# A hybrid decoder step on one core: expert weights in 2 MiB transfers of 16 KB per partition, a ring of 8 places, and a gather of full height

## The reference

```python
def expert_block(args):
    xb, e = args
    g = jnp.minimum(xb @ lp['w_gate'][e] + lp['b_gate'][e], SWIGLU_LIMIT)
    u = jnp.clip(xb @ lp['w_up'][e] + lp['b_up'][e], -SWIGLU_LIMIT, SWIGLU_LIMIT)
    act = g * jax.nn.sigmoid(SWIGLU_ALPHA * g) * (u + 1.0)
    return act @ lp['w_down'][e] + lp['b_down'][e]
```

## Time and profile before

| what | us |
|---|---|
| median of 3 runs (1362.7 to 1371.55) | 1368.54 |
| the profiled execution | 1360.56 |
| its span, first to last instruction | 1358.5 |

### The profile page before, as it was taken

The page is one execution under the profiler, slowest core; times in us unless marked ns, Lnnn a source line. Parts: engine busy times, 40 slices in busy tenths (PEclk is TensorE's granted clock), DMA queues, the critical chain, the costliest instruction groups (busy, mean ns, idle before and its releaser), DMA issues.

```text
span 1358.5 us, 15076 instructions
## 1 busy us (share of the span) xinstructions
PE 1278.8 (94%) x5901; PEld 588.4 (43%) x5902; DVE 316.2 (23%) x674; ACT 154.6 (11%) x253; POOL 35.2 (3%) x43
## 2 busy tenths in 40 slices
PE   5999979789999999999999999999999999999895
PEld 2653646454343534434353444434343434434332
DVE  2232462422021202112120211212120211112114
ACT  1331231210110001001000101000000101000001
POOL 0010232000000000000000000000000000000000
PEclk8899987868999999999999999999999999999988
DMA  9354767509899999999999999999999999999971
GB/s 375 155 195 135 279 240 292 228 12 407 352 410 408 409 409 409 409 410 410 409 409 410 410 409 409 410 410 409 410 410 410 409 410 409 409 409 409 410 295 40
DMA packets 125029, 477.53 MB, mean 352 GB/s; under 512 B 7360, under 2 KB 9536, under 8 KB 124736
## 3 DMA queue, kind: packets, MB, share of 16 engines
q1 hardware_dynamic: 124672, 474.41, 88.2%
q0 software_dynamic: 320, 2.60, 0.5%
HBM read 473.07 MB, written 3.91 MB: 351 GB/s over the span
## 4 chain that ended last, share of the span: by engine, by line
PE 81%; DMA 13%; DVE 3%; ACT 2%; issue 1%; DVEq 0%; ACTq 0%
PE ps L508 80%; DMA arena<-in_w_up 11%; ACT arena L1081 2%; DVE arena L1137 1%; DMA arena<-in_w_in 1%; DMA arena<-in_w_ada 1%; PE ps L856 0%; DMA arena<-in_xT 0%; PE ps L746 0%; DVE arena L1566 0%; DVE arena L1344 0%; DVE arena L1143 0%; DVE arena L1341 0%; DVE arena L1564 0%; PE ps L790 0%
## 5 line engine op out<-in xcount | busy, mean ns | idle before, releaser
L508 PE MATMUL ps<-arena 128*64 128x512 f32 (+7 forms) x5648 | 1244.3, 527 | 64.2 <-DVE arena L1137 24.3
L508 PEld LDWEIGHTS ps<-arena 128*64 128x64 f32 (+2 forms) x5648 | 557.0, 159 | 741.7 <-issue 625.1
L1081 ACT ACTIVATE arena<-ps 128x1024 f32<-128x1024 f32 x51 | 52.3, 1025 | 635.1 <-PE ps L508 618.1
L1137 DVE TENSOR_TENSOR arena<-arena,ps 128x320 f32<-128x320 f32 (+2 forms) x140 | 69.1, 494 | 162.6 <-PE ps L508 156.6
L1447 DVE TENSOR_SCALAR arena<-ps 128x1024 f32<-128x1024 f32 x17 | 20.8, 1224 | 348.3 <-PE ps L508 348.3
L1137 DVE TENSOR_TENSOR arena<-arena 128x1024 f32<-128x1024 f32 (+12 forms) x90 | 75.0, 858 | 79.0 <-ACT arena L1009 32.5
L1451 DVE TENSOR_SCALAR arena<-ps 128x1024 f32<-128x1024 f32 x17 | 20.8, 1225 | 207.7 <-PE ps L508 207.7
L1089 ACT ACTIVATE arena<-arena 128x1024 f32<-128x1024 f32 x17 | 18.0, 1060 | 281.9 <-DVE arena L1447 281.9
L1432 DVE TENSOR_SCALAR arena<-arena 128x64 f32<-128x64 f32 (+1 forms) x102 | 24.4, 305 | 1.8 <-issue 1.8
L1439 DVE COPY arena<-arena 128x64 f32 (+1 forms) x34 | 5.4, 193 | 78.1 <-PE ps L508 78.1
L821 PE MATMUL ps<-arena 128*128 128x128 f32 x136 | 19.2, 286 | 2.7 <-DVE arena L1452 2.7
(11 more groups left out here) (119 smaller groups left out, 155.0 us busy)
## 6 DMA issues: line engine op xcount, KB each, us to landing
arena<-in_w_gate SPq DMA_DIRECT2D x136, 1024.0 KB, 18.3
arena<-in_w_up SPq DMA_DIRECT2D x136, 1024.0 KB, 18.3
arena<-in_w_down SPq DMA_DIRECT2D x136, 1024.0 KB, 18.4
arena<-in_w_ada SPq DMA_DIRECT2D x24, 1024.0 KB, 7.6
arena<-in_w_in SPq DMA_DIRECT2D x10, 1024.0 KB, 11.7
arena<-in_w_out SPq DMA_DIRECT2D x4, 1024.0 KB, 8.0
arena<-in_s0T SPq DMA_DIRECT2D x1, 2048.0 KB, 9.6
out_ssmsT<-arena POOLq DMA_DIRECT2D x1, 2048.0 KB, 6.5
```

Of the source, the lines that this page charges most:

```text
L508: return pe.matmul(o, l, r, start=start, stop=stop, skip_group_check=True)
L1081: A(moe[name].rearrange("p (a b) -> p a b", a=2), ps[:, bank:bank + 2, :], ACT.Copy).then_inc(done, 1)
L1137: return V.tensor_tensor(o, a, b, op)
```

## The change

Three things change. The weights are laid out on the host so that each load is one contiguous piece per partition: 8 KB for a front unit (`w_front`), 16 KB for an expert load (`w_exp`). An expert load is now 2 MiB, half of a matrix, four chunks of 128 rows (CHUNKS); the ring has 8 places instead of 16, of the same 16 MiB, PER is 12, and a product waits for its loads, and frees them, in two halves instead of four quarters. And the gather's third tile is 128 rows high: the rows above 64 of `htok` and `sel` are set to zero once, by GpSimd at its start and by DVE before the router's result.

```diff
 UNIT = 2048
-RING = 16
 FS = 6
-PER = 24
+CHUNKS = 4
+LOAD = CHUNKS * D
+RING = 8
+HELD = FS * UNIT // LOAD
+PER = 3 * 2 * KC // CHUNKS
...
-        ring, ring_at = sb([RING, UNIT])
+        ring, ring_at = sb([RING, LOAD])
+        front = view(ring_at, [FS, UNIT])
...
         def exp_slot(j, k):
-            return (FS + PER * j + k) % RING
+            return (HELD + PER * j + k) % RING

         def exp_source(k, e):

-            m, p = k // 8, k // 2 % 4
-            return w_exp[m][bass.ds(e(k % 2), 1), :, 2 * p:2 * p + 2, :].rearrange("e p c n -> p (e c) n")
+            return w_exp[bass.ds(e(k % 2), 1), k // 2].rearrange("e p n -> p (e n)")
...
-                slot = ring[:, u % FS, :]
-                src = front_source(m, j)
-                sp.dma_start(slot.rearrange("p (c n) -> p c n", c=src.shape[1]), src).then_inc(front_landed[u % FS], 16)
+                sp.dma_start(front[:, u % FS, :], w_front[u]).then_inc(front_landed[u % FS], 16)

             def load_unit(k, e, slot):
-                sp.dma_start(ring[:, slot, :].rearrange("p (c n) -> p c n", c=2), exp_source(k, e)).then_inc(exp_landed[slot], 16)
+                sp.dma_start(ring[:, slot, :], exp_source(k, e)).then_inc(exp_landed[slot], 16)
...
                 for k in range(KC):
-                    for t, (t0, n) in enumerate(TILES):
-                        last = mm(ps[:, 6 + k // 4, (k % 4) * P:(k % 4 + 1) * P], htok[0:n, t, k * P:(k + 1) * P],
-                                  moe["sel"][0:n, t, :], t == 0, t == NT - 1)
+                    for t in range(NT):
+                        last = mm(ps[:, 6 + k // 4, (k % 4) * P:(k % 4 + 1) * P], htok[:, t, k * P:(k + 1) * P],
+                                  moe["sel"][:, t, :], t == 0, t == NT - 1)
                 last.then_inc(x_mm, 1)
...
-                for p in range(4):
+                for p in range(KC // CHUNKS):
                     for s in range(2):
                         pe.wait_ge(exp_landed[slots[2 * p + s]], loads[2 * p + s])
-                    w = [ring[:, slots[2 * p + s], :].rearrange("p (c n) -> p c n", c=2) for s in range(2)]
-                    for kk in range(2):
+                    w = [ring[:, slots[2 * p + s], :].rearrange("p (c n) -> p c n", c=CHUNKS) for s in range(2)]
+                    for kk in range(CHUNKS):
...
-                                if kk == 1 and half == 1:
+                                if kk == CHUNKS - 1 and half == 1:
                                     last.then_inc(exp_used, 1)
...
             pe.wait_ge(htok_ready, NT)
+            pe.wait_ge(pad_zero, 1)
             gather(0)
...
+            step(V.memset(moe["sel"][TS:P, 2, :], 0.0))
             step(V.memset(logit, 0.0))
...
                     if not last:
-                        dve.wait_ge(exp_used, q * PER + 17)
+                        dve.wait_ge(exp_used, q * PER + 2 * PER // 3 + 1)
                         pick_bias(lambda s: (q + 1) * 2 + s)
...
             step(Q.memset(line[:, :, 0:PAD], 0.0))
+            Q.memset(htok[TS:P, 2, :], 0.0).then_inc(pad_zero, 1)
+            pool.wait_ge(pad_zero, 1)
...
+    w_exp = np.stack([a[n][0] for n in ("w_gate", "w_up", "w_down")], axis=1)
+    w_exp = w_exp.reshape(NE, PER // 2, CHUNKS, P, D).transpose(0, 1, 3, 2, 4).reshape(NE, PER // 2, P, LOAD)
```

More of the change, by code:

```diff
@@ L282, in scratch @@
             up[0] += n
-            assert up[0] <= ring_at + RING * UNIT
+            assert up[0] <= ring_at + RING * LOAD
             return view(at, shape)
@@ L385, in build @@
         moe_zero = sem("moe_zero")
+        pad_zero = sem("pad_zero")
         sel_ready, selw_ready, pick_ready, x_mm, x_ready = (
@@ L393, in build @@
         dve_steps, act_steps, pool_steps = sem("dve_steps"), sem("act_steps"), sem("pool_steps")
[L395 to L410, removed]
+        w_front = d["w_front"]
+        w_exp = d["w_exp"]
         def exp_slot(j, k):
-            return (FS + PER * j + k) % RING
+            return (HELD + PER * j + k) % RING
         def exp_source(k, e):
-            m, p = k // 8, k // 2 % 4
-            return w_exp[m][bass.ds(e(k % 2), 1), :, 2 * p:2 * p + 2, :].rearrange("e p c n -> p (e c) n")
+            return w_exp[bass.ds(e(k % 2), 1), k // 2].rearrange("e p n -> p (e n)")
         def there(eng, i):
@@ L437, in load_front @@
             def load_front(u):
-                m, j = FRONT[u]
                 if u >= FS:
                     sp.wait_ge(front_used, u - FS + 1)
-                slot = ring[:, u % FS, :]
-                src = front_source(m, j)
-                sp.dma_start(slot.rearrange("p (c n) -> p c n", c=src.shape[1]), src).then_inc(front_landed[u % FS], 16)
+                sp.dma_start(front[:, u % FS, :], w_front[u]).then_inc(front_landed[u % FS], 16)
             def load_unit(k, e, slot):
-                sp.dma_start(ring[:, slot, :].rearrange("p (c n) -> p c n", c=2), exp_source(k, e)).then_inc(exp_landed[slot], 16)
+                sp.dma_start(ring[:, slot, :], exp_source(k, e)).then_inc(exp_landed[slot], 16)
             def load_first(v):
-                load_unit(v % PER, lambda s: 2 * (v // PER) + s, (FS + v) % RING)
+                load_unit(v % PER, lambda s: 2 * (v // PER) + s, (HELD + v) % RING)
             for u in range(NF):
@@ L457, in _ @@
                     sp.dma_start(s0T, d["s0T"]).then_inc(ld_s0, 16)
-            for v in range(RING - FS):
-                begins, ends = ring_at + (FS + v) * UNIT, ring_at + (FS + v + 1) * UNIT
+            for v in range(RING - HELD):
+                begins, ends = ring_at + (HELD + v) * LOAD, ring_at + (HELD + v + 1) * LOAD
                 if v == 0:
@@ L470, in _ @@
                 load_first(v)
-            for v in range(RING - FS, PER * UNROLL):
+            for v in range(RING - HELD, PER * UNROLL):
                 if v < RING:
-                    last = max(u for u in range(NF) if u % FS == v - (RING - FS))
+                    last = max(u for u in range(NF) if u % FS * UNIT // LOAD == v - (RING - HELD))
                     if last == NF - 1:
@@ L513, in unit @@
             def unit(u, c=2):
-                return ring[:, u % FS, :].rearrange("p (c n) -> p c n", c=c)
+                return front[:, u % FS, :].rearrange("p (c n) -> p c n", c=c)
             def mean_square(bank):
@@ L838, in product @@
                                 c = slice(s * CAP, (s + 1) * CAP)
-                                last = mm(ps[c, bank + half, :], rows[:, 2 * p + kk, c], w[s][:, kk, half * AW:(half + 1) * AW],
-                                          False, p == 3 and kk == 1)
-                                if kk == 1 and half == 1:
+                                last = mm(ps[c, bank + half, :], rows[:, CHUNKS * p + kk, c], w[s][:, kk, half * AW:(half + 1) * AW],
+                                          False, CHUNKS * p + kk == KC - 1)
+                                if kk == CHUNKS - 1 and half == 1:
                                     last.then_inc(exp_used, 1)
@@ L865, in pair @@
                 pe.wait_ge(pick_ready, q + 1)
-                product(0, 0, X, loads[0:8], slots[0:8])
+                product(0, 0, X, loads[0:PER // 3], slots[0:PER // 3])
                 if first:
@@ L870, in pair @@
                     wait(pe, comb_added, (q - (0 if serial else 1)) * KC)
-                product(1, 2, X, loads[8:16], slots[8:16])
+                product(1, 2, X, loads[PER // 3:2 * PER // 3], slots[PER // 3:2 * PER // 3])
                 if not serial:
@@ L884, in pair @@
                     pe.wait_ge(more_read, 1)
-                product(2, 4, A, loads[16:24], slots[16:24])
+                product(2, 4, A, loads[2 * PER // 3:PER], slots[2 * PER // 3:PER])
             nf = PASSES - 1
@@ L1445, in activate @@
                 g, s = moe["g"], moe["s"]
-                dve.wait_ge(exp_used, q * PER + 8)
+                dve.wait_ge(exp_used, q * PER + PER // 3)
                 V.tensor_scalar(halves("g"), blocks(0), LIMIT, None, ALU.min).then_inc(g_ready, 1)
@@ L1449, in activate @@
                 step(tt(g, g, s, ALU.mult))
-                dve.wait_ge(exp_used, q * PER + 16)
+                dve.wait_ge(exp_used, q * PER + 2 * PER // 3)
                 step(V.tensor_scalar(halves("s"), blocks(2), LIMIT, -LIMIT, ALU.min, ALU.max))
@@ L1658, with unit, front_unit @@
     row = np.concatenate([a[n].reshape(1, -1) for n in ("g_v_a", "dt_bias", "a_log", "d_skip", "b_router")], axis=1)
+    def unit(w, c, columns):
+        return feat(w.T).transpose(2, 1, 0)[:, c, columns].reshape(P, UNIT)
+    def front_unit(m, j):
+        two, four = slice(2 * j, 2 * j + 2), slice(4 * j, 4 * j + 4)
+        if m.startswith("ada"):
+            s = int(m[3:])
+            return unit(a["w_ada"][0], two, slice(s * D, (s + 1) * D))
+        if m == "xbc":
+            return unit(a["w_in"][0], two, slice(3 * AW, 3 * AW + D))
+        if m == "uv":
+            return unit(a["w_in"][0], two, slice(0, 2 * AW))
+        if m == "z":
```

(7 more changed lines are left out.)

## The result

The changed kernel takes 1312.92 us (median of four runs, 1311.35 to 1317.04); the kernel before, on the same chip, 1365.62 (1359.71 to 1371.55). The forecast span was 1321.6.

What follows compares the result with a forecast made beforehand. DMA was taken to bound the kernel, 61.4 us per pair against PE's 59.4. Start 345.2, losses 4.9, loads 844.7 and tail 126.8 gave span 1321.6; 36.9 us off the median gave 1331, range 1308 to 1356.

Steps and rivals of the forecast that it cites:

- tail behind the last up piece of pair 15: PE, ACT and DVE work ending the span: 123.15 + 3.4 - 3.1 + 3.3 = 126.8 us.
- What bounds: In the pair loop, DMA at 58.9 us per pair would still set the pace, above PE's 56.3.
- The rate: Expert loads in 16 KB pieces: 427 GB/s instead of 409.6, bounded by 373 and 440.
- rival of half the gain: Expert loads reach only 419 GB/s, so 344 MiB take 860.9 us and the kernel 1348 us; chance 0.12.
- The gather: All 24 matmuls at full height take 5.35 us instead of 8.45, 3.1 less per pair, not paid out in the steady part.
- rival with the gather no cheaper: PE's 59.4 us per pair exceed DMA's 58.9, so PE binds all through: 1350 us; chance 0.05.
- Gather of pair 0 runs at 1.2 GHz: Before the pair loop's continuous loads: 14.96 us becomes 10.7 at the low clock, so 4.0 us earlier (0 to 4.3).
- the reference point: First transfer issued after DMA's standstill, when part of pair 0's down product frees its places: from 349.81 to 345.2 us.
- the 3.4 of the release: A product first frees places after four chunks instead of two, so the issue after DMA's standstill comes 3.4 us later.
- The front: Loads ahead of the pairs, in 8 KB instead of 4 KB pieces, save 0.9 us (0 to 1.5).
- PE's longer wait: Mid-up, once per pair, 2.6 us; the lowered clock then loses 3.3 us, counted once, after pair 15.
- The ring: After the last up piece lands, DMA has 39.3 us of work, next release after 27.7: 11.6 us of cover.

Runs made afterwards that it cites:

- experiment 1: The kernel before, with 4 KB pieces and 16 places, and only the gather's third tile made 128 rows high; 1345.9 us, ratio 0.985.
- experiment 2: The changed kernel with the gather's third tile back at 64 rows, keeping 16 KB pieces and 8 places; 1344.02 us, ratio 0.985.
- experiment 4: The changed kernel with the same 2 MiB transfers, but each partition's row cut into four pieces of 4 KB; 1349.51 us, ratio 0.990.
- Experiment 6: The changed kernel with six of the eight ring places used, 12 MiB, 4 MiB lying unused; 1353.0 us, ratio 0.991.

## Why the prediction was right

The parts of the forecast span, set against the trace of the changed kernel, in us:

| part | forecast | trace |
|---|---|---|
| start of pair 0's gather | 278.3 | 283.3 |
| from there to the first issue after the standstill | 66.9 | 57.6 |
| 344 MiB | 844.7 at 427 GB/s | 842.0 at 428.4 |
| latency, small losses | 4.9 | 5.4 |
| tail behind the last up piece of pair 15 | 126.8 | 126.5 |
| span | 1321.6 | 1314.8 |

- *What bounds.* DMA, after three turns of PE; the two limits of 56.3 and 58.9 us came out at 56.49 and 58.75. Experiments 1 and 2 show them one at a time.
- *The rate.* 427 from four microseconds of s0T was good to 0.3%, and of the stretches bounding it neither 373 nor 440 was. That it is the piece per partition, and not the transfer's size, is shown by experiment 4. The Trainium skill ("DMA: Bandwidth & Descriptors", Why small descriptors are slow) has the form of the law right, a fixed cost per packet, but the about 3 cycles it states do not reach here: by an estimate with these cycles, scaled from the 4 KB row, 2, 8 and 16 KB would give 400, 414 and 417 GB/s, and 387, 422 and 428 were measured. The rival of half the gain, 419 GB/s, fell with it.
- *The gather.* 5.35 us were forecast, and the steady one takes 5.46, from its first weight load to the first transpose behind it (434.06 to 439.52; before, by the same measure, 746.24 to 754.70, 8.46). Its two lines stand below. As argued, its 3 us are not paid out where DMA binds (experiment 1's loop), but they are the reason why the faster transfers can be used at all: without them experiment 2 stops at 59.4. That last part I had only as a rival with the gather no cheaper, at 1350 us; it measured 1344.
- *Pair 0: the term that was mis-sized.* "Gather of pair 0 runs at 1.2 GHz" was wrong, and with it the 4.0 us ahead of the reference point. The way from the gather's start to the first issue became 13.0 us shorter (70.6 to 57.6), not 3.7. The 3.1 of pair 1's gather and the 3.4 of the release came out within 0.1. But pair 0's gather, with the six records behind it, went from 15.54 to 8.89 us, 6.6 in place of 4.0, and 6.8 that the sum did not have came from the products behind it: the granted clock there was 0.85 before (294.71 to 342.98) and is 1.00 now (292.21 to 330.75). Experiment 1 gives the gather's whole share as 16.3, experiment 2 the release's as +3.4; 16.3 - 3.4 = 12.9. All eight kernels with the full-height gather raise the clock within pair 0's gather, which takes 7.4 to 8.9 us; the two with 64-row tiles do not, and take 15.5.
- *The front.* It was to end 0.9 us earlier and ended 4.2 later. The 0.9 itself came out: PE's first long stretch begins at 41.31 us before and at 41.27 in experiment 1, both held up by a load in 4 KB pieces that ends 0.35 us ahead, and between 40.14 and 40.48 in the eight kernels with 8 KB pieces. What came on top is the clock in the front: the same 176 records took 20.23 us before, at a granted 0.92, and 23.44 in the changed kernel, at 0.78, and such differences stand between executions with the same front. So pair 0's gather starts anywhere from 277.2 to 285.8 us in the ten executions read.
- *PE's longer wait.* Forecast once per pair, 2.6 us, with 3.3 us of clock behind it, hidden in the next turn. It is 2.04 us, costs 1.70 where the clock falls at all, and is hidden as said. After pair 15 the clock did not fall there (12.66 us at 1188.48); instead pair 16 ran slower, gate and up 33.17 us together for 31.65, down 18.00 for 17.12, and the last 16 records 7.30 for 6.28, 3.4 in all. The tail's sum is right, but one of its terms is in another place, so that it fits is partly luck.
- *The ring.* With 8 places DMA never stops, as forecast, but the cover is smaller than 11.6 us: 39.3 us of work against 28.7 without a release in a turn where the clock fell (27.0 where it did not), less the restart, so about 8. Experiment 6 is where that error shows.

The lines of the gather and of the front, the changed kernel's gather first, then the stretches of the front before and now:

```profile
434.06 5.43 PEld L495 LDWEIGHTS ps<-arena 128*128 128x128 f32 x48 [0.81 <-issue]
...
439.52 1.04 PE L808 MATMUL ps<-arena 128*128 128x128 f32 x8
```

```profile
41.31 104.75 PE ps L508 x378
...
149.97 20.23 PE ps L508 x176
```

```profile
40.45 105.33 PE ps L495 x378
...
149.68 23.44 PE ps L495 x176
```

Two errors of opposite sign, the front's 5.0 us and pair 0's 9.3, partly hid each other in the sum, which is luck; the rest of the 18 us to the median lies between one profiled execution and the next, since the forecast was counted down from a median of 1368.54 and the changed kernel's profiled run is 4 us above its own.

## What to carry to other kernels

Where two resources are nearly full, find the time of one turn on each; a saving on one is worth only the distance to the other, and two parts of a change can earn more together than alone. Choose the contiguous piece per partition by the cost per packet, and the number of places by the longest stretch without a release plus the restart of the queue: here 16 KB for 4 KB was worth 37 us, and two places fewer cost 40.

## What the runs showed of the hardware

- By the rates a packet costs 9.4 ns of a DMA engine beside 37.66 ns per KB, from 2 to 16 KB per packet (387 to 428 GB/s); the 1213 ns of a 32 KB packet lie on the same line.
- Twenty-four matmuls, a third of them 64 rows high, take 8.46 us, and all at 128 rows 5.46, although they multiply more. What costs is not the 64 rows but each change of height. Within a tile of either height the weight loads of the mixed gather (from 746.24) start 0.11 us apart, and 0.31 us apart at each of its 15 changes: 15 x 0.20 = 3.0 us, the whole difference. At 1.2 GHz the pauses show in the timeline of pair 0's gather before (in brackets the pause ahead):

```profile
279.14 0.93 PEld L508 LDWEIGHTS ps<-arena 128*128 128x128 f32 x4 [2.13 <-issue]
280.29 0.50 PEld L508 LDWEIGHTS ps<-arena 64*128 64x128 f32 x2 [0.22 <-issue]
281.02 0.93 PEld L508 LDWEIGHTS ps<-arena 128*128 128x128 f32 x4 [0.23 <-issue]
```

  The Trainium skill ("TensorEngine Tiling (Array Packing)", Key Properties) says that a change of the tiling mode drains TensorE; the pauses at the changes of height agree with that, though the traces show the pause and not its cause.
- PE counted as busy for 100% of pair 0's mixed gather and stayed at 1.2 GHz; with the full-height one, whose weight loads follow without a gap (5.00 of 5.00 us, not 3.88), it rose to 2.4 GHz before the gather was over.
- A wait of about 2.04 us once per turn sometimes brought the clock down (599.69 and 834.67, with 2.05 and 2.03 us) and sometimes not (775.93, with 2.04). A longer one need not: in experiment 4 each turn has a wait of 3.15 us, and the granted clock is 1.00 in its loop.

```profile
606.92 12.64 PE L496 MATMUL ps<-arena 128*64 128x512 f32 x80 [3.15 <-DMA arena<-in_w_exp]
```

  So the length of a wait alone did not decide it; what else did, no run here shows.
